# Five pieces of a modulation product moved from the attention part into the dense layer

## The reference

```
for l in (0, 1):
    mod = silu(c) @ ada_w[l] + ada_b[l]              # 1024 -> 6*1024, one row per stream
    sh1, sc1, g1, sh2, sc2, g2 = split(mod, 6)
    o = token_mixer(rms_norm(x, norm1_g[l]) * (1 + sc1) + sh1)
    x = x + g1 * o
    x = x + g2 * channel(rms_norm(x, norm2_g[l]) * (1 + sc2) + sh2)

token_mixer: xn @ w_in -> group A (attention), group B (mLSTM), group C (latent attention)
             -> concatenation @ w_out
channel:     layer 0 (silu(x @ w1) * (x @ w3)) @ w2, the dense layer; layer 1 the top 2 of 8 experts
```

## Time and profile before

| | us |
|---|---|
| median of 3 runs | 1607.78 |
| lowest and highest | 1603.17, 1608.71 |
| the profiled execution | 1598.65 |
| its span, first to last instruction | 1597.1 |
| PE busy in the span | 1516.1 (95%) |
| DVE busy | 1164.3 (73%) |
| ACT busy | 917.1 (57%) |

### The profile page before, as it was taken

How to read it: one execution, slowest core, us unless ns; L and a number is a source line. 1 busy time by engine, 2 the same in 40 slices (tenths; PEclk the granted TensorE clock), 3 DMA queues, 4 the chain that set the end, 5 groups by cost and what they waited for, 6 DMA issues and landing times.

```text
span 1597.1 us, 19723 instructions
## 1 busy us (share of the span) xinstructions
PE 1516.1 (95%) x7058; PEld 1163.8 (73%) x7058; DVE 1164.3 (73%) x1222; ACT 917.1 (57%) x791; POOL 70.7 (4%) x113
## 2 busy tenths in 40 slices
PE   6898879999999788999999999999999999999998
PEld 3454447888655556788888888888888888888876
DVE  1364554444536655888888888888888888888998
ACT  1213234344232432777777777777777777777774
POOL 1510000000001000000000000000000000000200
PEclk9999989999999897999999999999999999999999
DMA  9979968865695475999999999999999999999994
GB/s 360 323 205 417 389 223 256 280 211 185 224 322 192 154 286 210 358 377 366 399 374 365 394 378 378 379 381 373 384 378 372 389 376 373 380 381 362 391 403 158
DMA packets 192825, 523.26 MB, mean 328 GB/s; under 512 B 10880, under 2 KB 71456, under 8 KB 187656
## 3 DMA queue, kind: packets, MB, share of 16 engines
q1 hardware_dynamic: 167440, 493.39, 83.3%
q0 software_dynamic: 7024, 18.63, 3.5%
q10 hardware_dynamic: 18312, 10.60, 2.3%
HBM read 505.50 MB, written 17.08 MB: 327 GB/s over the span
## 4 chain that ended last, share of the span: by engine, by line
PE 83%; DVE 6%; ACT 5%; DMA 3%; issue 3%; SPq 0%; DVEq 0%; ACTq 0%
PE PS L617 21%; PE PS L619 21%; PE PS L618 21%; PE PS L732 5%; PE PS L623 4%; DVE parts L2061 3%; PE PS L947 2%; DMA ring<-in_ada_w 2%; PE PS L698 2%; PE PS L637 1%; ACT parts L1454 1%; PE PS L762 1%; PE PS L746 1%; DMA ring<-in_w_in 1%; ACT arena L1291 1%
## 5 line engine op out<-in xcount | busy, mean ns | idle before, releaser
L2061 DVE TENSOR_TENSOR parts<-ring,parts 128x2048 fp32r<-128x2048 f32 x336 | 765.5, 2290 | 103.6 <-ACT parts L1454 100.9
L1454 ACT ACTIVATE parts<-ring 128x2048 fp32r<-128x2048 f32 x336 | 644.2, 1920 | 218.3 <-PE PS L619 218.3
L617 PE MATMUL PS<-parts 128*128 128x512 f32 x1608 | 634.6, 395 | 8.5 <-DVE parts L2061 4.1
L619 PE MATMUL PS<-parts 128*128 128x512 f32 x1608 | 628.1, 391 | 0.0
L618 PE MATMUL PS<-parts 128*128 128x512 f32 x1608 | 627.5, 390 | 0.0
L617 PEld LDWEIGHTS PS<-parts 128*128 128x128 f32 x1608 | 302.6, 188 | 76.5 <-DVE parts L2061 9.3
L619 PEld LDWEIGHTS PS<-parts 128*128 128x128 f32 x1608 | 302.4, 188 | 64.5
L618 PEld LDWEIGHTS PS<-parts 128*128 128x128 f32 x1608 | 302.9, 188 | 61.8 <-issue 0.2
L1614 DVE TENSOR_TENSOR parts<-ring,parts 128x2048 fp32r<-128x2048 f32 x33 | 75.5, 2289 | 53.0 <-PE PS L619 50.2
L732 PE MATMUL PS<-ring,xnT 128*128 128x420 f32 (+1 forms) x240 | 92.2, 536 | 0.0
L1232 ACT ACTIVATE parts<-ring 128x2048 fp32r<-128x2048 f32 x33 | 63.0, 1915 | 29.9 <-PE PS L619 29.9
(11 more groups left out here) (314 smaller groups left out, 935.1 us busy)
## 6 DMA issues: line engine op xcount, KB each, us to landing
ring<-in_moe_w SPq DMA_DIRECT2D x336, 1024.0 KB, 7.0
ring<-in_ada_w SPq DMA_DIRECT2D x40, 1024.0 KB, 7.5
ring<-in_w_in SPq DMA_DIRECT2D x32, 840.0 KB, 10.8
ring<-in_ffn_w SPq DMA_DIRECT2D x44, 512.0 KB, 5.4
ring<-in_w_out SPq DMA_DIRECT2D x16, 1024.0 KB, 8.7
ring<-in_ffn_w SPq DMA_DIRECT2D x11, 1024.0 KB, 4.8
expert_rows<-zeros ACTq DMA_DIRECT2D x17, 512.0 KB, 4.9
ring<-in_ada_w SPq DMA_DIRECT2D x16, 512.0 KB, 11.7
```

The lines of the kernel that those rows point to most:

```text
L617: mm(out, s_hi, m_hi, start=start, stop=False)
L619: return mm(out, s_lo, m_hi, start=False, stop=stop)
L1454: A(w_hi(j), slot(n), ACT.Copy).then_inc(hi_ready, 1)
L2061: TT(w_lo(j, 3), slot(W0 + j), w_hi(j).bitcast(f32), ALU.subtract).then_inc(split_done, 1)
```

## The change

Layer 0's order has 22 `a` in place of 27. The last five pieces of chunk 3 go into the dense layer: the four `rows_of` behind the transposes of stream 1 (`norm_T(0, 1, 1)`), the transposes of the rows behind `up(0, 1, 1)`. Their four loads of 1 MB now stand between those of stream 1's output projection and those of the dense layer. DVE does `rows_out` ahead of the dense layer's loop and `columns_out` in its first turn. PE waits for the turned columns before `up(1, 0, 1)`, since the bank is shared. The three orders of both layers are laid anew around this. ACT issues a bias load behind the dense layer that it issued in the mixer. The diff, with a line or two of the tables:

```
+LATE = 5
 PE_ORDER = [x.split() for x in ("""
...
-A1 A1 a B1 B1 a o0 B1 a a B1 o0 B1 a a C1 C1 C1 a a o0 o0 a a a C1 C1 a a o0 C1 C1 a
+A1 A1 a B1 B1 o0 a B1 a a B1 o0 B1 a a C1 C1 C1 a a o0 o0 a C1 C1 C1 o0 C1
...
-            early_of.append(g_ada)
+            early_of.append(g_ada + (l == 0))
...
             if l == 0:
+                for k in range(KD - (LATE - 1), KD):
+                    ada_load(g_ada, k)
+                g_ada += 1
                 def w2_load(f):
...
                 if s == 1:
-                    wait("turned_out", early_of[l])
+                    wait("turned_out", early_of[l] - (l == 0))
...
                 up(0, 0, 0)
                 up(0, 1, 0)
                 norm_T(0, 1, 1)
+                for _ in range(LATE - 1):
+                    next(ada)
                 wait("xs_ready", 2)
                 up(0, 0, 1)
                 up(0, 1, 1)
+                next(ada)
                 for f in range(1, N_FF):
                     up(f, 0, 0)
+                    if f == 1:
+                        wait("turned_out", early_of[0])
                     up(f, 0, 1)
...
                     dense_ffn()
+                    for _ in range(LATE):
+                        next(ada)
...
                     if f + 1 < N_FF:
                         split_lo(first["up", f + 1, 0])
+                    if f == 0:
+                        next(ada)
...
                 if l == 0:
-                    dense_ffn()
+                    for _ in range(LATE - 1):
+                        next(ada)
+                    dense_ffn(ada)
```

More of the change, by code:

```diff
@@ L362, in build_program @@
                     g_after_1.append(g_ada)
-            early_of.append(g_ada)
-            assert at_piece["i1"] == 9 and at_piece["o0"] == 4 and at_piece["a"] % 9 == 8
+            early_of.append(g_ada + (l == 0))
+            assert at_piece["i1"] == 9 and at_piece["o0"] == 4 and (at_piece["a"] + LATE * (l == 0)) % 9 == 8
             assert [at_piece[x] for x in ("A0", "A1", "B0", "B1", "C0", "C1")] == [3, 3, 4, 4, 6, 6]
@@ L959, in mixer, with dense_ffn @@
                         next(pieces[token])
-            def dense_ffn():
+            def dense_ffn(ada):
                 def up(f, half, s):
```

23 lines of the change are left out of this document (12 added, 11 removed).

## The result

The changed kernel took 1613.86 us in the median (14 runs), the kernel before 1605.44 on the same chip (14 runs). The ratio is 1.0069, with a 95% interval of 1.0048 to 1.0090. The change makes the kernel slower by 0.7%, some 11 us (8.4 us between the medians). The forecast was 1613.7, from a higher starting point: +5.9 us on 1607.78.

What follows compares the result with a forecast made beforehand. PE and DMA both looked full late in layer 0's mixer, with the end hanging on PE's chain with VectorE and ScalarE. Terms -0.5 + 2.6 - 0.9 + 5.7 - 2.0 + 0.5 + 0.5 = +5.9 on 1607.78 gave 1613.7 us, range 1603.5 to 1620.

Steps and rivals of the forecast that it cites:

- the clock terms: Layer 0: half-clock changes at the mixer's end, -0.9 us, and before stream 1's first dense unit, -2.0 us.
- the ring: Start of layer 0's dense layer: first dense load issued late for lack of a slot, delaying ScalarE's split, +5.7 us.
- nothing on top: Dense layer's start: the next two dense loads are split by 233, before ScalarE is needed at 236.5, adding no time.
- The projection piece behind the transposes: End of layer 0's mixer: the piece, now ahead of the products with v, lengthens the chain by +2.6 us.
- the start of the mixer's end: Layer 0's mixer: two pieces leave ahead of the 16 transposes, so that step starts earlier, -0.5 us.
- The clock at the mixer's end: Layer 0: half clock hits transposes (+1.4) and projection piece (+1.9), full clock returns behind (-4.2); taken as -0.9 us.
- The rival in which it stays low: Half clock holds from the transposes through the products with v: +11.9 us, 1619.7; chance 0.20.
- The four pieces: Layer 0's dense layer: 3.7 us of pieces fill PE's 4.08 us wait before stream 1's first unit, costing nothing.
- the clock kept behind them: Stream 1's first dense unit: pieces keep PE busy, so some ten matmuls escape half clock, -2.0 us.
- The dense layer passes a delay on: Layer 0's dense layer, bound by PE, passes any delay at its start on whole.
- Transfers pace the mixer: Rival for layer 0's mixer: four loads fewer take 10.8 us off, giving -4.9 us, 1602.9; chance 0.08.
- Part 4, layer 1: Layer 1: an input-projection unit moved ahead of small products delays VectorE's chain, +0.5 us, bounds -0.4 and +1.9.

Runs made afterwards that it cites:

- after_same: The changed kernel run again unaltered, beside the kernel before in another set of runs: 1610.85 us, ratio 1.0073.
- ring_hold: Kernel before, with SP holding the first three dense loads back until stream 1's projection pieces 2, 3 and 4 are used: 1610.52 us, ratio 1.0051.
- late3_old: Kernel before with only three pieces moved, its orders otherwise kept less layer 0's last three modulation tokens: 1603.01 us, ratio 1.0010.
- l0_new: The changed kernel with layer 1's three orders put back as before: 1614.70 us, ratio 1.0068 to the kernel before.
- late5_old: All five pieces moved, but with the orders of the kernel before less layer 0's last five modulation tokens: 1610.77 us, ratio 1.0069.
- fill_only: Kernel before with 16 spare matmuls of a piece's shape in PE's wait before stream 1's first dense unit: 1593.39 us, ratio 0.9986.
- l1_new: Kernel before with only layer 1's three orders replaced by the changed kernel's: 1609.82 us, ratio 1.0052.
- after_fill_l1: The changed kernel with 4 and 14 spare 128-column matmuls in two waits of layer 1's mixer: 1606.55 us, ratio 1.0044 to the kernel before.
- fill_l1: Kernel before with 4 and 14 spare 128-column matmuls in two PE waits of layer 1's mixer: 1600.35 us, ratio 1.0017.

## Why the prediction was right, and where it was not

The median came 0.2 us from the forecast, the rise (8 us by medians, 11 by the ratio) was larger than the 5.9 forecast, from a start 2.3 us lower. The closeness is luck: the rise was about half of what the ratio says, and the lower start made up for it. The fixed terms had been summed to -0.5 + 2.6 + 5.7 + 0.5 + 0.5 = +8.8 and measured +6.4; the clock terms to -0.9 - 2.0 = -2.9, and measured +5.9 in the set of after_same, with an error of 2.0. Its largest term, the ring, held in mechanism and nearly in size; the clock terms had the wrong sign, in both layers.

- **The ring (+5.7): right**, in mechanism and nearly in each stamp (issue forecast at 218.7, split at 223.4): issue at the end of the second projection piece (219.53), landing and split 5 us on, the normalised input behind it. ring_hold alone gives 6.2 us in the stage. What the step did not foresee is that the new gap also brings half clock to the first dense unit (2.1 of the 6.2 us, so that 4.1 are the wait itself, for the +5.7); and the next loads do show (ScalarE waits 0.77 and 1.52 us for them), so "nothing on top" was a little too kind. The Trainium skill, "DMA: Bandwidth & Descriptors", section "Rules for kernel authors", asks for early issue and a late wait; ring_hold and late3_old agree: three loads held back cost 0.5%, and with two pieces fewer moved no cost can be told.
- **The projection piece behind the transposes (+2.6), the start of the mixer's end (-0.5): order right, size not shown.** The products stood directly behind the piece, 4.9 us later than in the earlier trace rows, of which some 1.2 us was lost before 170 us. l0_new and late5_old differ in this place and by 0.2 us fixed, with an error of 0.6; their profiles differ by 1.8 us from the latents' up-projection to the transposes of `o` (41.44 against 39.59).
- **The clock at the mixer's end (-0.9): right in kind in this profile.** The transposes took 2.82 (forecast 2.9; the working written there gives +1.2, not +1.4, and they took +1.3), the piece 4.41 (5.6), and 4.15 of the 4.2 us behind came back: -2.15 us in all. The rival in which it stays low did not occur in this profile: the 24 products took 2.79, not 3.9.
- **The four pieces (0), the clock kept behind them (-2.0): right in this stage.** 0.23 us apart from the start, and in fill_only, with nothing else changed, the same. But the first dense unit, which now begins at half clock, takes the same 2 us away again.
- **The dense layer passes a delay on: not tested.** Layer 1's first transposes came 5.5 us later (435.99 against 430.49; forecast 5 to 6), but at 435.88 in l1_new with nothing changed ahead of them, and at 442.05 in after_same with the program unaltered.
- **Transfers pace the mixer (1602.9): wrong**, though four loads less did lower the demand (the DMA share up to 200 us fell from 0.97 to 0.94). Between 160 and 215 us PE waits for no weights in either profile; it idles 5.47 us for ScalarE instead.
- **The steps that failed: "Part 4, layer 1", +0.5 with bounds -0.4 and +1.9, and the clock terms -0.9 and -2.0 as the clock of layer 0's whole change.** In layer 1 the late small products were there and cost 1.7 us fixed, in place of +0.5. But the term held only this wait, and its bounds no clock at all: l1_new shows 20 us more at half clock, +7.2 us with an error of 1.4. For layer 0, l0_new shows +4.4 and ring_hold +4.0, each with an error of 1.7 or less, where the forecast had -2.9. It had treated the clock as a matter of the two places that it looked at; in those two the profile agrees, and the time at half clock came elsewhere.

**Open.** Of late5_old's +6.2 fixed, ring_hold explains 4.2, and 2.0 with an error of 0.8 has no experiment; late3_old (+0.2) says only that it comes with the fourth and fifth piece. Why layer 0's change alone, or layer 1's new orders alone, brings more half clock isn't known either: the low stretches move between executions, and the fills were put into two waits at once.

## What to carry to other kernels

Before work is moved past a ring of buffers, count places, not microseconds: as long as the slot of the next consumer's first load is freed by work that is already done, the load comes in time (three pieces, 1.0010, not told from none); once it has to wait for work just ahead of that consumer, the load is late, and everything in the queue behind its first reader too (five pieces, 1.0069). Put such a reader behind whatever in its queue doesn't need the load. And where a low clock is about, measure many runs and record the granted clock of each: the part of a difference that goes with the clock can then be estimated, with its error. What was worth having of this move, a filled wait, could be had without it.

## What the runs showed of the hardware

The same program spent from 3.0% to 6.8% of its span at 1.2 GHz on one chip (mean granted clock 0.985 to 0.966 in the 35 runs of the kernel before beside the second four kernels), and by the fit each us of that cost 0.36 us, not 0.5. In the profiles most stretches at half clock lie in the two mixers, where PE has short waits, and one in layer 1 of the changed kernel's profile covered the whole of this window, although PE was busy 25.69 of its 28 us:

```profile
530.00:558.00 28.00, 25.69 (x116) 21.53 (x115) 11.92 (x43) 8.99 (x31) 0.00 (x0) 0.50 0.02 9
```

The Trainium skill, "TensorE: Matmul & The Clock Gate", section "What's actually happening", has activity lift the clock; by this row much work on PE went by without such a lift. after_fill_l1 agrees with the rule in its direction (21.5 us less at half clock), fill_l1 shows nothing (0.3 us more), and for foretelling a single stretch it was of little help here.
